# Squares of the last two tiles summed by TensorE, and an earlier root, in the norms at the entry of four stages

## What is computed

```python
def _rmsnorm(x, g):
    xf = x.astype(jnp.float32)
    y = xf * lax.rsqrt(jnp.mean(xf * xf, axis=-1, keepdims=True) + EPS)
    return (y * g.astype(jnp.float32)).astype(x.dtype)
...
        x = x + _rmsnorm(h, post_mix_g[layer])
        h = _swiglu(_rmsnorm(x, pre_ffn_g[layer]), ffn_w_gate[layer], ffn_w_up[layer], ffn_w_down[layer])
        x = x + _rmsnorm(h, post_ffn_g[layer])
```

## Time and profile before

| | us |
|---|---|
| median of 3 runs | 4180.58 (4179.37 to 4186.12) |
| profiled execution | 4175.23 |
| its span | 4173.4 |
| TensorE busy | 3898.7 (93%) |
| VectorE busy | 2679.8 (64%) |
| ScalarE busy | 1449.4 (35%) |
| GpSimd busy | 1202.5 (29%) |

### The profile page before, as it was taken

One profiled execution on the slowest core, in us unless ns is written; L12 is line 12 of the kernel. 1 busy time (PEld: TensorE's weight loads), 2 busy tenths in 40 slices (PEclk: granted clock), 3 DMA queues, 4 the chain that ended last, 5 costly groups with the idle time before them and its releaser, 6 DMA issues.

```text
span 4173.4 us, 47439 instructions
## 1 busy us (share of the span) xinstructions
PE 3898.7 (93%) x18382; PEld 3094.4 (74%) x18382; DVE 2679.8 (64%) x3001; ACT 1449.4 (35%) x1896; POOL 1202.5 (29%) x583
## 2 busy tenths in 40 slices
PE   8999899999879999989999988998999989998988
PEld 6557788877656666778887867886788878876777
DVE  6764787889764554378778988531655555546783
ACT  4334432234333333243223433212333333325512
POOL 2002134445413333213444531222222112212054
PEclk9999999999989999999999999998999989999999
DMA  3002223345320000222334532223211221323054
GB/s 110 20 16 81 101 91 104 96 153 189 115 76 21 21 26 21 86 101 87 113 104 158 172 119 105 98 101 113 83 62 54 71 76 61 110 73 106 22 206 141
DMA packets 130874, 382.36 MB, mean 92 GB/s; under 512 B 13460, under 2 KB 14104, under 8 KB 125400
## 3 DMA queue, kind: packets, MB, share of 16 engines
q1 hardware_dynamic: 130648, 379.32, 27.4%
HBM read 278.08 MB, written 101.19 MB: 91 GB/s over the span
## 4 chain that ended last, share of the span: by engine, by line
PE 71%; DVE 21%; ACT 4%; issue 1%; DMA 1%; POOL 1%; SPq 0%; DVEq 0%; ACTq 0%; POOLq 0%
PE ps L359 22%; PE ps L1389 20%; PE ps L454 7%; PE ps L872 3%; PE ps L2875 2%; PE ps L2881 2%; PE ps L4342 2%; PE ps L2182 1%; DVE acc L1658 1%; PE ps L2174 1%; DVE top L1562 1%; DVE xop L1562 1%; PE ps L2936 1%; DVE x L636 1%; PE ps L2862 1%
## 5 line engine op out<-in xcount | busy, mean ns | idle before, releaser
L312 POOL TENSOR_TENSOR wlo<-wraw,whi 128x1024 fp32r<-128x1024 f32 x185 | 455.7, 2463 | 1764.8 <-ACT whi L304 1630.9
L1389 PE MATMUL ps<-xop,whi 128*128 128x512 f32 x1984 | 616.7, 392 | 15.5 <-DVE acc L1683 10.1
L304 ACT ACTIVATE whi<-wraw 128x1024 fp32r<-128x1024 f32 x185 | 196.0, 1060 | 907.6 <-PE ps L359 626.4
L1389 PE MATMUL ps<-top,whi 128*128 128x512 f32 x1488 | 470.0, 397 | 22.3 <-DVE acc L1652 17.0
L1389 PEld LDWEIGHTS ps<-xop,whi 128*128 128x128 f32 x1984 | 372.2, 188 | 100.2 <-DVE acc L1683 12.6
L1389 PE MATMUL ps<-xop,wlo 128*128 128x512 f32 x992 | 387.7, 391 | 0.0
L454 PE MATMUL ps<-xhalf,whi 128*128 128x512 f32 x1024 | 363.6, 437 | 4.8 <-ACT n L4056 3.5
L1389 PEld LDWEIGHTS ps<-top,whi 128*128 128x128 f32 x1488 | 281.5, 190 | 91.1 <-DVE acc L1652 20.3
L359 PE MATMUL ps<-xhi,whi 128*128 128x512 f32 x900 | 322.9, 441 | 23.2 <-DVE xlo L656 6.7
L1784 POOL TENSOR_TENSOR wlo<-wsum,whi 128x1024 fp32r<-128x1024 f32 (+2 forms) x102 | 229.4, 2249 | 368.0 <-ACT whi L1414 367.4
L1389 PE MATMUL ps<-top,wlo 128*128 128x512 f32 x744 | 294.5, 396 | 0.0
(11 more groups left out here) (625 smaller groups left out, 7424.7 us busy)
## 6 DMA issues: line engine op xcount, KB each, us to landing
wraw<-in_w_dram SPq DMA_DIRECT2D x185, 512.0 KB, 3.7
h_keep<-h SPq DMA_DIRECT2D x154, 256.0 KB, 4.8
wraw<-in_s_dram SPq DMA_DIRECT2D x48, 512.0 KB, 4.2
f<-h_keep SPq DMA_DIRECT2D x24, 768.0 KB, 5.7
wmore<-in_s_dram SPq DMA_DIRECT2D x32, 512.0 KB, 4.2
x_keep<-x SPq DMA_DIRECT2D x16, 1024.0 KB, 3.9
g_keep<-gates SPq DMA_DIRECT2D x64, 256.0 KB, 2.4
gb<-g_keep SPq DMA_DIRECT2D x32, 512.0 KB, 3.6
```

The costliest lines, as they stand in the source:

```text
L304: se.own().activation(K.hi(c), K.raw[:, c % NRAW, :], ACT.Copy).then_inc(*K.S(("hi", c)))
L312: ge.own().tensor_tensor(K.lo(c), K.raw[:, c % NRAW, :], K.hi(c).bitcast(F32), SUB).then_inc(*K.G(("lo", c)))
L1389: d = pe.e.matmul(out[:, s, :], w[:, o], x[:, i, :], start=(j < 3 and i == 0 and t == 0), stop=(i == k - 1 and t == 2), skip_group_check=True)
```

## The change

The column sums of an entry that follows a residual take three parts: the accumulator after add 5, and the squares of tiles 6 and 7 as they are; adds 6 and 7 are gone there. VectorE makes low(6) ahead of update and residual 7. In the mixer (e2) and the hybrid block (e4) the root is made by ScalarE and VectorE, and the row is turned ahead of step 7 (`back_first`); ScalarE's and VectorE's waits for the stage's start stand behind it. In e1 and e3 root and order of the row stay. `high_first` waits for the high part of the weights first, for the low part ahead of its second half. In the feed-forward's end ScalarE makes the weight splits ahead of its last squares and GpSimd doesn't wait for the last add.

```diff
@@ high_first
         for (c, o), b in zip(blocks, pairs):
-            pe.wait_ge(*K.at("lo", c))
+            pe.wait_ge(*K.at("hi", c))
...
     pe.wait_ge(*K.at(*low))
     for (c, o), b in zip(blocks, pairs):
+        pe.wait_ge(*K.at("lo", c))
@@ (also renamed at its other call, in mix_out_tensor)
-def two_columns_tensor(pe, K, n, *parts):
+def more_columns_tensor(pe, K, n, *parts):
...
-            d = pe.e.matmul(K.ps[:, b, k:k + 1], x[:, part(k)], K.ones[:, 0:1], start=(i == 0 and k == 0), stop=(i == 1 and k == 7), skip_group_check=True)
+            d = pe.e.matmul(K.ps[:, b, k:k + 1], x[:, part(k)], K.ones[:, 0:1], start=(i == 0 and k == 0), stop=(i == len(parts) - 1 and k == 7), skip_group_check=True)
@@ enter_vector
-    for i in range(1, 7):
+    for i in range(1, 6):
         if Y is not None:
             update(i + 1)
             residual(i + 1)
         low(i)
         add(i)
-    add(7)
+    low(6)
+    if Y is not None:
+        update(7)
+        residual(7)
+    else:
+        add(6)
+        add(7)
     low(7)
@@ entry_tensor
-    columns_tensor(pe, K, N.name, N.acc)
-    next(product)
+    if N.after is None:
+        columns_tensor(pe, K, N.name, N.acc)
+    else:
+        more_columns_tensor(pe, K, N.name, (N.acc, (N.name, "add", 5)), *((N.sq[i % 2], (N.name, "sq", i)) for i in (6, 7)))
+    if not back_first:
+        next(product)
     stat_back_tensor(pe, K, N.name, N.sq[0])
@@ new
+def entry_scalar(se, K, N):
+
+    steps = wide_walk(se, K, weights_scalar, 8, 3)
+    for _ in range(5):
+        next(steps)
+    root_scalar(se, K, N.name)
+    next(steps)
+    settle_scalar(se, K, N)
+    for _ in steps:
+        pass
@@ ffn_lead_scalar
-        se.wait_ge(*K.at(N.name, "add", 7))
+        se.wait_ge(*K.at(N.name, "sum"))
@@ ffn_scalar
     square_quarter(se, K, F, NB - 1, 3, (NB - 1, 0))
-    square_quarter(se, K, F, NB - 1, 2, (NB - 2, 1))
-    square_quarter(se, K, F, NB - 1, 1, None, (slice(0, 1), slice(1, 2)))
     se.wait_ge(*K.at(n, "p", NB - 1, 5))
     weights_scalar(se, K, F.c0 + 4)
     se.wait_ge(*K.at(n, "p", NB - 1, 6))
     weights_scalar(se, K, F.c0 + 5)
+    square_quarter(se, K, F, NB - 1, 2, (NB - 2, 1))
+    square_quarter(se, K, F, NB - 1, 1, None, (slice(0, 1), slice(1, 2)))
@@ ffn_gpsimd
-    ge.wait_ge(*K.at(n, "sum", 1))
@@ mixer1_tensor (hybrid_in_tensor alike)
-    entry_tensor(pe, K, M.N, [("m1 gates", 0), (("p", 0), 0), (("p", 0), 1)])
+    entry_tensor(pe, K, M.N, [("m1 gates", 0), (("p", 0), 0), (("p", 0), 1)], back_first=True)
@@ mixer1_vector (hybrid_in_vector: settle_vector becomes root_vector)
-    ve.fence(K, "m1 start")
+    ve.reach("m1 start")
+    root_vector(ve, K, M.N.name, M.N.sq[0], D)
+    ve.after(K, "m1 start")
     ve.kept(K, "m1")
-    settle_vector(ve, K, M.N)
@@ mixer1_scalar (hybrid_in_scalar: entry_steps becomes entry_scalar)
-    se.fence(K, "m1 start")
+    se.reach("m1 start")
+    entry_scalar(se, K, M.N)
+    se.after(K, "m1 start")
     se.kept(K, "m1")
-    entry_steps(se, K, weights_scalar, 3, lambda se, K: settle_scalar(se, K, M.N))
@@ mixer1_gpsimd and hybrid_in_gpsimd: settle_gpsimd is gone
```

More of the change, by code:

```diff
@@ L679, in enter_gpsimd, with entry_tensor @@
     weights_gpsimd(ge, K, ge.block // 8 + 2)
-def entry_tensor(pe, K, N, tiles, sums_at=7, given=()):
+def entry_tensor(pe, K, N, tiles, sums_at=7, given=(), back_first=False):
     product = wide_tensor(pe, K, tiles, N.xs, (N.name, "high half"))
@@ L1169, in mix_out_tensor @@
         pass
-    two_columns_tensor(pe, K, n, (O.ysq, (n, "add", 6)), (O.sq[1], (n, "sq", 7)))
+    more_columns_tensor(pe, K, n, (O.ysq, (n, "add", 6)), (O.sq[1], (n, "sq", 7)))
     stat_back_tensor(pe, K, n, O.sq[0])
@@ L2429, in mixer1_gpsimd @@
     ge.kept(K, "m1")
-    entry_steps(ge, K, weights_gpsimd, 3, lambda ge, K: settle_gpsimd(ge, K, M.N))
+    entry_steps(ge, K, weights_gpsimd, 3, lambda ge, K: None)
     for j in range(4):
@@ L2538, in hybrid_in_tensor @@
     pe.reach("hy start")
-    entry_tensor(pe, K, H.N, [("h0", 0), ("h0", 1), ("hp", 0)])
+    entry_tensor(pe, K, H.N, [("h0", 0), ("h0", 1), ("hp", 0)], back_first=True)
     project2_drive(chain((0,), dense_tensor(pe, K, "hp", H.N.xs, NP, first=1)), lambda m: None, small_rows_tensor(pe, K, H))
@@ L2549, in hybrid_in_vector @@
     ve.reach("hy start")
-    settle_vector(ve, K, H.N)
+    root_vector(ve, K, H.N.name, H.N.sq[0], D)
     ve.after(K, "hy start")
@@ L2592, in hybrid_in_scalar @@
     se.reach("hy start")
-    entry_steps(se, K, weights_scalar, 3, lambda se, K: settle_scalar(se, K, H.N))
+    entry_scalar(se, K, H.N)
     se.after(K, "hy start")
@@ L2614, in settle @@
     def settle(ge, K):
-        settle_gpsimd(ge, K, H.N)
         ge.after(K, "hy start")
```

## The result

The changed kernel is slower, as forecast: median 4203.8 us of four runs against 4180.0 of four of the kernel before, ratio 1.0058, 95% interval 1.0043 to 1.0072. That is +23.8 us where the forecast's sum gave +29.8. The profiled execution has a span of 4201.5 us.

A forecast was written before the change was run, and what follows sets the result against it. The prediction took TensorE to bound the kernel (71% of the chain, VectorE 21%). Its terms, 7.4 + 6.3 + 6.2 + 7.1 for the entries and 2.8 for the tails, sum to 29.8 us on 4180.6: 4210.4 us, range 4188 to 4226.

The forecast's parts named there:

- e4: Hybrid's entry: 16.45 us from the sums' start to the restart in place of 9.35, no wait left, +7.1 us.
- e3: Second feed-forward's entry: as the first's 7.4 us, less the 1.12 that low(6) ahead of update(7) removes, +6.3 us.
- +1.6: Run of 48 sums in an entry: clock falls 3.6 us in, leaving 14 slower instructions, +1.6 us, bounds 0 and 5.7.
- +2.4: Wide matmuls behind the 48 sums run at half speed until the clock returns, +2.4 us, from 1.75 to 3.0.
- e2, the step that failed: Mixer's entry: forget row 8.5 us later, less 2.28 us of TensorE's wait for softplus, +6.2 us.
- Moving low(6) gains nothing at the other three: All entries but the second feed-forward's: early low(6) gains 0, as step 6 follows step 5 there.
- they are off the path at e2: Mixer's entry: VectorE's two last adds, 2.56 us, run while TensorE is in step 5; nobody waits for them.
- The tails: Two feed-forward ends: +2.2 us from later squares, spread's 1.45 back, adds held by GpSimd's splits; 1.4 each, 2.8 us.
- Full clock: Rival, all four entries: the clock never falls in the sums, +11.9 us, 4192.5 us; chance 0.14.
- Slow all through: Rival, entries: clock falls 2 us into each run, returns after 6 us; near +41, 4221.6 us; chance 0.10.
- No effect: Rival, whole kernel: waits and split order change nothing on the path, the rest cancels, within 0.2%; chance 0.06.
- VectorE is what the entries wait for: Rival, entries: TensorE idles ahead of low(6), sums fall in idle time, −9.8 us, 4170.8 us; chance 0.08.

The follow-up runs named there:

- Wide in place: Kernel before, with 14 redundant wide matmuls added ahead of the 16 column sums in each of the four entries: 4183.0 us, ratio 1.0011.
- sums thin: Changed kernel with each entry's sums in six runs of 8; at mixer's and hybrid's entry row behind step 7, root on GpSimd: 4204.2 us, ratio 1.0064.
- before again: The kernel before with no edit, timed and profiled once more: 4180.6 us, ratio 1.0005.
- tails back: Changed kernel with the feed-forward's end as before: ScalarE's last squares ahead of its weight splits, GpSimd's last split behind the last add: 4195.7 us, 1.0042.
- order only: Changed kernel with adds 6 and 7 back on VectorE, 16 sums an entry, and the feed-forward's end as before: 4177.8 us, ratio 0.9997.
- adds: Changed kernel with adds 6 and 7 back on VectorE and 16 one-column sums an entry, not 48: 4179.2 us, ratio 1.0003.
- after again: The changed kernel with no edit, timed and profiled once more: 4201.3 us, ratio 1.0055.
- sums spread: Changed kernel with the same 48 sums an entry, the accumulator's 16 ahead of step 6, the other 32 ahead of step 7: 4200.1 us, 1.0062.

## Why the prediction was right, and where it was not

*The sums.* The count was right: 32 more an entry at 0.105. The clock was right in kind and near in size. At e1 the 48 took 5.78 us and step 7 2.64 more: 6.7 for 7.4. There it fell 4.7 us after the first sum, not 3.6, so the term "+1.6" was 0.7 (5.78 less 48 x 0.105) and "+2.4" was 2.6. At e3 it fell 3.7 us after the first sum; the 48 took 6.72 and step 7 5.96, so both terms were 1.7. In the 16 unbroken runs of 48 of the four traces the fall came 3.7 to 5.2 us after the first sum. At e1 and e3 the place hardly changed the sum, as what a later fall saves in the sums it adds to step 7: from the sums on each lost 6.7 to 6.8 in all four traces, of which 3.4 is count and the rest is clock. Wide in place (3.2 an entry) shows the first without the second. e3 as a whole is 5.3 for 6.3, since the moved low(6) gained 1.5 ahead of the sums.

By the rule of the Trainium skill (TensorE: Matmul & The Clock Gate, why this matters) that was set against the earlier trace rows, no idle gap would mean no fall. The trace does not agree: in the stretches from 494 to 500 above TensorE is busy without a gap and the clock falls. Nor is a wait behind narrow work enough by itself: in sums thin the clock fell within a wait of 2.54 us at e1 and stayed at e3 through one as long.

*e2, the step that failed.* The term was 6.2, the entry lost 2.2. Three things make it up. First, "Moving low(6) gains nothing at the other three", and "they are off the path at e2" of the two adds, rested on the earlier trace rows, an execution in which steps 5 and 6 ran partly at 1.2 GHz. At full clock TensorE waits there (1.17 in before again). From the entry's start to the sums took 44.4 us in that trace (1195.91 - 1151.52) and 41.6 after (1199.85 - 1158.26): 2.8 that I had at nothing. Before again has the sums' row 42.9 after its start, where the first trace has 44.2 in the same view, so some 1.4 of this is clock and 1.4 the order. Second, the sums took 6.00 and not 6.64, since the clock fell 4.5 us after the first of them (1204.16) and not 3.6, and step 7 took 5.11 and not 6.65, since part of the slow time had passed in the wait for the root and in the transposes. Third, the rest was right: 1.28 us from the sums to the transposes for 1.18, 1.94 for 1.97, and the wait ahead of y went. Counted from the sums' start, as the forecast was, the forget row came 6.5 us later (15.6 for 9.0), not 8.5; counted from the entry's start 3.7 (57.2 for 53.4), and the product with y 1.1. Between it and 1250 the changed kernel spends some 2 us more at 1.2 GHz, hence 2.2.

*e4.* 7.1 forecast, 4.7 and 5.8 measured. The restart was without a wait, 14.3 us after the sums' start, 4.9 more than before, for the forecast 16.45; again the sums (5.7 for 6.64) and step 7 (5.2 for 6.65) were the terms that were too large. The wait for the root, 1.29, was near the 1.18 charged.

*The tails.* 1.4 each forecast, 1.4 to 1.6 measured (tails back against changed, order only against adds). The forecast's parts are all there in the first tail: the 16 sums wait 2.24 us longer (5.58 for 3.34), the spread gives 1.45 back, and the held adds make TensorE wait 0.8 longer (from the start of the 16 sums to that of the next 8 it is 4.22 us for 3.44). That is 1.6. In the tail of order only, where the splits start at 1142.39, the same two adds take 1.42 us; in the changed kernel's timeline they take 3.46:

```profile
1139.44 1.42 DVE L1619 TENSOR_TENSOR t<-t,sqa 128x512 f32<-128x512 f32 x2
...
1142.39 4.87 POOL L312 TENSOR_TENSOR wlo<-wraw,whi 128x1024 fp32r<-128x1024 f32 x2 [15.50 <-DVE t L1619]
```

The Trainium skill's page SBUF — State Buffer (SBUF: two separate sides) has one of VectorE and GpSimd keep the port pair that they share for a whole instruction while the other, where its instruction needs the pair, blocks. The rows agree with it: what is lost (2.0 of the adds, 1.5 to 2.1 of a spread) stays within the length of one split, 2.4.

*The root on ScalarE* brought no table load into an entry, as taken. The first matmul of the kernel starts at 7.29 for 8.71 and of that gain 0.1 us is left by 69, as taken. In after again 1.3 us are left there, while before again is 0.6 later than the first trace, so whether the start is worth nothing or the forecast's bound of 1.2 is not settled. No run tried the wait on high halves alone.

*The whole.* An estimate from these terms: count 4 x 3.36 = 13.4, clock (334 and 333 us at 1.2 GHz less 302 and 313, halved) 13.0, tails 3.0, the two new waits for the root 2.6 (1.28 at e2, 1.29 at e4), less the waits that went (2.28 at e2, 2.39 at e4, 1.12 at e3, and 1.0 at e2 ahead of the product behind the forget row, 2.51 for 3.49) and 1.4 of order at e2: 23.8, for 22.8 and 23.8 measured. That it meets the second to the digit is luck: the clock term is a difference of traces that differ by 11 us among themselves. The trace alone would have said 28 (4201.5 - 4173.4); some 6 of that is the low hybrid of one trace. The forecast was 6 us too high since its four entries were too dear, 27.0 for 19.0 to 20.1.

*The rivals.* Full clock: refuted by the rows above. Slow all through: the clock fell 3.7 us after the first sum or later, not 2, and the time is below its 4221.6. No effect: refuted by the ratio, 1.0058, and with the 32 sums taken out (adds) it is back at 1.0003. VectorE is what the entries wait for: refuted as the outcome, and yet the mechanism that the e2 term lacked. It has its place at full clock, as at e2 in before again and, for 1.17 us at step 6, at e1 in wide in place, and I had counted it only at e3.

## What to carry to other kernels

One-column sums on TensorE are dear beyond their count. At e1 and e3 the 32 more took 3.4 us, and the half clock in and behind the run of 48 cost another 3.4; where TensorE waited anyway, at e2 and e4, part of it was hidden. Runs of 8 between wide matmuls kept the clock through the sums, a run of 32 kept it at one entry of four in sums spread. Where two engines are nearly level, which of them is late depends on the clock of that one execution, so look at the granted clock of the stretch, or at a second trace, before an engine is called off the path. When two traces are compared, count from the last instruction that both programs share, not from the start of the stage. And taking work out of the way of one instruction pays only as far as it does not land on another: the weight split that was moved from the root fell on the spread, and the removed wait for low(6) turned up as a wait for the root.

## What was not expected of the hardware

Two executions of the kernel before agree within 0.4 us in the six stretches and differ by 2.9 and 6.3 in two others (1250 to 1797, 2640 to 4140), with 11 us more at 1.2 GHz over the whole. A narrow run of 3.4 us kept the clock at e3 and lost it at e1, e2 and e4 in one and the same execution. The fall within a run of 48 came 3.7 to 5.2 us after its first instruction, and yet the run and step 7 behind it lost the same 6.7 to 6.8 us at e1 and e3 in all four traces. Two copies of 512 columns that take 0.89 us alone took 2.34 to 2.99 beside a GpSimd split, in three places.
